# A decoder trunk on one core: the recurrence's decay computed from a tanh, and the order of the work around it

## What is computed

```
h = x * (1 + scale) + shift
proj = h @ w_in[l]                       # a_b a_c a_x a_g | q k v b_g | c_x c_g | d_u d_g
y_a = a_b * causal_dwconv(a_c * a_x) * silu(a_g)
y_b = dilated_attention(q, k, v, rel_bias) * silu(b_g)
y_c = rglru_branch(c_x, ...) * silu(c_g)
y_d = s5_branch(d_u, ...) * silu(d_g)
y = concat(y_a, y_b, y_c, y_d) @ w_out[l]
x = layer_norm(ALPHA * x + (1 + gate) * y)
```

```
r  = sigmoid(xh @ wa + ba);  ig = sigmoid(xh @ wx + bx)
log_a = -8 * r * softplus(-lam)
a = exp(log_a);  mult = sqrt(-expm1(2 * log_a))
h_t = a_t * h_(t-1) + mult_t * ig_t * xc_t
```

## Time and profile before

| | |
|---|---|
| Time, median of 3 runs | 1796.57 us (1792.95 to 1797.87) |
| The profiled execution | 1796.57 us, span 1794.8 us |
| Busy share of the span | TensorE 93%, its weight loads 72%, VectorE 68%, ScalarE 43%, POOL 13% |
| Mean granted clock of TensorE | 0.962 of full |
| First step of the loop of layer 0 and of layer 1: VectorE's start | 144.25 and 978.42 us |
| VectorE's start of the later steps, layer 0 | 299.37, 451.88, 605.27 us |
| VectorE's start of the later steps, layer 1 | 1135.47, 1286.36, 1437.29 us |

### The profile page before, as it was taken

The page is one execution under the profiler, slowest core; times in us unless marked ns, Lnnn a source line. Parts: engine busy times, 40 slices in busy tenths (PEclk is TensorE's granted clock), DMA queues, the critical chain, the costliest instruction groups (busy, mean ns, idle before and its releaser), DMA issues.

```text
span 1794.8 us, 23025 instructions
## 1 busy us (share of the span) xinstructions
PE 1666.7 (93%) x7527; PEld 1294.2 (72%) x7527; DVE 1219.8 (68%) x2338; ACT 774.2 (43%) x1022; POOL 233.3 (13%) x281
## 2 busy tenths in 40 slices
PE   2339999999999999999998999999999999999995
PEld 1327778777777777768886777877877777776884
DVE  5884894796688479657862576488468558743758
ACT  2125554653544555421127554554555464532120
POOL 2132111111111111000005111111111111100000
PEclk9559999999999999999997999999999999999998
DMA  7999889989988988858736788978988888855322
GB/s 255 369 349 254 212 208 241 231 222 229 222 223 209 237 227 213 237 166 292 224 121 178 178 187 205 221 185 188 218 198 195 198 203 193 186 166 206 134 95 104
DMA packets 322942, 376.05 MB, mean 210 GB/s; under 512 B 27064, under 2 KB 224032, under 8 KB 319784
## 3 DMA queue, kind: packets, MB, share of 16 engines
q1 hardware_dynamic: 294632, 272.36, 47.2%
q0 software_dynamic: 28224, 102.77, 31.9%
HBM read 261.81 MB, written 10.51 MB: 152 GB/s over the span
## 4 chain that ended last, share of the span: by engine, by line
PE 84%; DVE 8%; DMA 4%; ACT 2%; SPq 1%; issue 1%; POOL 0%; DVEq 0%; ACTq 0%; POOLq 0%
PE bank L970 19%; PE bank L977 19%; PE bank L971 18%; PE bank L1014 18%; DMA w_lo<-raw 3%; DVE work L1337 3%; DVE ada_acc L1337 2%; PE bank L860 2%; PE bank L994 2%; PE bank L890 1%; DVE y_t L1337 1%; PE bank L916 1%; PE bank L904 1%; PE bank L868 1%; PE bank L878 1%
## 5 line engine op out<-in xcount | busy, mean ns | idle before, releaser
L970 PE MATMUL bank<-op_hi,w_hi 128*128 128x512 f32 x1536 | 617.6, 402 | 0.0
L971 PE MATMUL bank<-op_lo,w_hi 128*128 128x512 f32 x1536 | 602.4, 392 | 0.0
L977 PE MATMUL bank<-op_hi,w_lo 128*128 128x512 f32 x1536 | 382.7, 391 | 7.4 <-DMA w_lo<-raw 7.4
L604 ACT ACTIVATE w_hi<-raw 128x1024 fp32r<-128x1024 f32 x196 | 207.8, 1060 | 399.1 <-PE bank L971 248.5
L970 PEld LDWEIGHTS bank<-op_hi,w_hi 128*128 128x128 f32 x1536 | 290.3, 189 | 94.2 <-issue 34.3
L977 PEld LDWEIGHTS bank<-op_hi,w_lo 128*128 128x128 f32 x1536 | 288.1, 188 | 71.6 <-DMA w_lo<-raw 12.2
L971 PEld LDWEIGHTS bank<-op_lo,w_hi 128*128 128x128 f32 x1536 | 290.4, 189 | 59.9 <-issue 1.9
L556 POOL DMA_DIRECT2D w_lo<-raw x196 | 170.9, 872 | 1056.2 <-ACT w_lo L607 1037.1
L607 ACT ACTIVATE w_lo<-raw 128x1024 fp32r<-128x1024 f32 x196 | 206.9, 1055 | 92.8 <-PE bank L977 92.7
L1337 DVE SCALAR_TENSOR_TENSOR ada_acc<-ada_in,cond,ada_acc 128x512 f32<-128x512 f32 (+1 forms) x234 | 181.5, 776 | 66.8 <-DMA ada_in<-in_w_ada 46.9
L744 ACT ACTIVATE w_hi<-raw 128x1024 fp32r<-128x1024 f32 x56 | 59.5, 1062 | 233.2 <-PE bank L1014 215.6
(11 more groups left out here) (226 smaller groups left out, 1568.5 us busy)
## 6 DMA issues: line engine op xcount, KB each, us to landing
w_lo<-raw POOLq DMA_DIRECT2D x196, 512.0 KB, 5.1
raw<-in_w_in SPq DMA_DIRECT2D x192, 512.0 KB, 4.4
ada_in<-in_w_ada SPq DMA_DIRECT2D x256, 256.0 KB, 4.4
raw<-in_w_out SPq DMA_DIRECT2D x64, 512.0 KB, 4.1
raw<-in_w_ada SPq DMA_DIRECT2D x27, 512.0 KB, 7.2
ada_in<-in_w_ada SPq DMA_DIRECT2D x18, 512.0 KB, 7.6
rot<-in_w_ada SPq DMA_DIRECT2D x10, 512.0 KB, 7.1
bias_t<-in_w_ada SPq DMA_DIRECT2D x9, 512.0 KB, 7.5
```

The costliest lines, as they stand in the source:

```text
L604: act.activation(w_hi[:, n % NHL, :], raw[:, n % NRAW, :], ACT.Copy).then_inc(s.hi_done.sem, 1)
L970: pe.matmul(o, w_hi[:, n % NHL, w], op_hi[:, k, :], start=k == 0, stop=False)
L971: mm = pe.matmul(o, w_hi[:, n % NHL, w], op_lo[:, k, :], start=False, stop=False)
L977: mm = pe.matmul(o, w_lo[:, n % NHL, w], op_hi[:, k, :], start=False, stop=k == KT - 1)
```

## The change

- ScalarE no longer computes the exponential. The square root of T goes to `lru_s[2]`, T itself stays in `lru_s[0]`.
- VectorE computes from T, with an addition, a reciprocal over 128x512, a product and one more `ts`: 1 / (1 + T), sqrt(T) / (1 + T) and a = 2 / (1 + T) - 1. The factor of `y_out(2)` goes from 0.25 to 0.5. The four columns of constants for the exponential go.
- TensorE: `s5_drive(3)` follows half-unit 13 instead of 14. It was put in the list ahead of the scores, so it runs before `scores(3)` there.
- VectorE's order: `s5_out(2)` comes before both `normalise`, an `ada` call between them, one more after `s5_scan(3)`; two calls near the end of the step go.
- SP: the S5 parameters of the next step are loaded behind everything of half 23 instead of at 22, and of the places for the conditioning's pieces one moves from 22 to 20 (the formula gives the same numbers for all others).

```diff
-ADA_AT = (1, 2, 4, 5, 7, 8, 10, 11, 13, 14, 16, 17, 19, 22, 22, 23)
-OWN_STEPS = (167, 166)
+ADA_PLACES = 16
+OWN_STEPS = (170, 169)
...
-                            if n == 22:
-                                s5_loads(step + 1)
-                        for place, at_half in enumerate(ADA_AT):
-                            if max(at_half, 2 - step) == n:
+                        for place in range(ADA_PLACES):
+                            if max(3 * place // 2 + 1, 1 + place, 2 - step) == n:
...
+                    if step < CT - 1:
+                        s5_loads(step + 1)
...
-                        act.activation(lru_s[2], lru_s[0], ACT.Exp, scale=lru_c[:, l, bass.ds(ct + 12, 1)],
-                                       bias=lru_c[:, l, bass.ds(ct + 12, 1)])
...
-                        act.activation(lru_s[0], lru_s[0], ACT.Sqrt).then_inc(s.from_act.sem, 1)
+                        act.activation(lru_s[2], lru_s[0], ACT.Sqrt).then_inc(s.from_act.sem, 1)
...
-                    for q, at in enumerate((5, 7, 10, 14)):
+                    for q, at in enumerate((5, 7, 10, 13)):
                         put(at, s5_drive, q)
...
                 dve.wait_ge(s.from_act.sem, s.from_act.at(2, ct))
-                own(stt(lru_s[0], lru_s[2], 1.0, lru_s[0], ADD, MUL), s.own)
+                own(ts(lru_s[0], lru_s[0], 1.0, ADD), s.own)
+                own(dve.reciprocal(lru_s[0], lru_s[0]), s.own)
+                own(tt(lru_s[2], lru_s[2], lru_s[0], MUL), s.own)
+                own(ts(lru_s[0], lru_s[0], 2.0, MUL, -1.0, ADD), s.own)
                 own(stt(lru_s[1], lru_s[1], 1.0, xc, ADD, MUL), s.own)
-                own(tt(lru_s[1], lru_s[1], lru_s[0], MUL), s.own)
-                own(dve.tensor_tensor_scan(xc, lru_s[2], lru_s[1], 0.0, MUL, ADD), s.own)
+                own(tt(lru_s[1], lru_s[1], lru_s[2], MUL), s.own)
+                own(dve.tensor_tensor_scan(xc, lru_s[0], lru_s[1], 0.0, MUL, ADD), s.own)
...
                 s5_scan(2)
                 ada(2, 1)
+                s5_out(2)
                 normalise(0)
+                ada(2, 1)
                 normalise(1)
-                s5_out(2)
                 own(silu2(0, "c_g", gx[:, 0, :]), s.own)
-                own(stt(y_out(2), xc, 0.25, gx[:, 0, :], MUL, MUL), s.gate_used[0])
+                own(stt(y_out(2), xc, 0.5, gx[:, 0, :], MUL, MUL), s.gate_used[0])
                 s5_in(3)
                 s5_scan(3)
+                ada(2, 1)
                 s5_out(3)
...
+
                 ada(2, 1)
-
                 own(silu2(0, "b_g", gx[:, 0, :]), s.own)
-                ada(2, 1)
-                ada(2, 1)
                 dve.wait_ge(s.pv_done.sem, s.pv_done.at(2 * ST, ct))
```

More of the change, by code:

```diff
@@ L172, in trunk @@
         s5c = sb("s5c", [P, DEPTH, 4, 16])
-        lru_c = sb("lru_c", [P, DEPTH, 16])
+        lru_c = sb("lru_c", [P, DEPTH, 12])
         glu_hb = sb("glu_hb", [P, DEPTH, 4])
@@ L1424, in preparation @@
                 own(ts(lru_c[:, :, 0:4], tmp[:, 3, :, 0:4], LRU_C / 4, MUL), sched)
-                own(ts(lru_c[:, :, 12:16], tmp[:, 3, :, 0:4], -LRU_C / 2, MUL), sched)
                 r = ROWS["lru_ba"][0]
```

## The result

The changed kernel takes 1821.8 us in the median of four runs (1820.3 to 1823.0) where the kernel before takes 1794.8 (1790.8 to 1797.9; the three runs of the table above and a fourth): a ratio of 1.0152, with a 95% interval of 1.0132 to 1.0172. It is 27 us slower. The forecast was 36.5 us slower (1833, range 1816 to 1848), so the measured time lies inside the range, in its lower part.

The account below looks back on a forecast made before the run. TensorE was taken as nearly always busy, with VectorE a hidden, almost level second bound in layer 0. Layer 0 23.8, layer 1 5.4, restarts 2.2 and clock 5.1 make 36.5 us on 1796.6: 1833, range 1816 to 1848.

Parts of the forecast that it names:

- The mechanism: In both layer loops, VectorE's later work makes TensorE wait where it needs VectorE's results: 1825 to 1841, chance 0.73.
- The wide reciprocal: VectorE's reciprocal over 512 columns, extrapolated from narrow rows: 3.35 us; net 4.3 us more on VectorE in each step.
- Layer 0: TensorE waits 1.7 after half 10, 1.25 after half 13, 3.0 after half 16: 5.95 us a step, 23.8 for four.
- Layer 1: TensorE waits 1.35 us a step before the second head's transposes after half 16: 5.4 us for four steps.
- The restart: Weights are not loaded ahead over a wait of TensorE: 16 waits x 0.14 = 2.2 us.
- The clock: Three of four waits of 3.0 us after half 16 are followed by a short fall to 1.2 GHz: 5.1 us.
- SP's queue: S5 loads behind the last half's loads, one ada place from half 22 to 20; TensorE doesn't wait there: 0.
- The cheap reciprocal: Rival: the wide reciprocal takes 0.43 us; layer 0 waits 13.4 us in all, layer 1 5.4: 1822, chance 0.08.
- That the clock falls at every wait: Rival: TensorE's clock falls at every wait, longer after the long ones, 20.4 us instead of 5.1: 1848, chance 0.12.
- The rival of a faster kernel: Rival: shifted loads relieve the start of a step, where w_lo came late, giving back 6.7 us: 1790, chance 0.03.

Follow-up runs that it names:

- the cheap reciprocal: The changed kernel with the reciprocal replaced by a multiplication with 0.5 over the same 128x512, which changes the recurrence's values: 1814.8 us, 1.0104 to the kernel before.
- the try: The kernel before with the S5 loads behind half 23 and the third and fourth ada places at halves 5 and 6 instead of 4 and 5: 1787.6 us, 0.9958.

## Why the forecast came out as it did

**The mechanism held.** VectorE is an almost level second bound in layer 0; TensorE waits for it at fixed meeting points. The new waits stand where they were forecast and nowhere else: after halves 10, 13 and 16 in layer 0, after half 16 in layer 1, none before the S5 outputs. The arithmetic alone, the order alone, and the changed kernel with the exponential back each show their own part of these waits.

**Term by term.**
- *The wide reciprocal:* 3.35 us from three narrow rows; measured 3.353. The slope of the rows held over 480 more columns. The Trainium skill ("VectorE: DVE Perf Modes", the walkthrough, fixed hardware budget) gives a repeat count of 8; taken as 8 cycles a column, that was an estimate of 4.3 us. The trace disagrees with that reading of it. (By the forecast's own steps it would have raised the sum by 0.9 us a step in layer 0, so by some 4 us and not by 6.)
- *Layer 0, forecast 5.95 us a step (1.7, 1.25, 3.0).* Measured 1.46, 0.83 and 2.77, so 5.06 where all three stand, 18.6 over four steps against 23.8. At the first bank release VectorE is 2.36 us late (365.45 against 355.55, with TensorE 7.54 later in the two traces), not 2.6, so the first wait is 0.2 shorter. Before the second, the kernel before had a pause of 0.48 us in VectorE's step, ahead of the first piece of the second ada chunk (371.90), and the changed kernel has none there. I had carried it over. In the first and the fourth step the second wait is missing: the clock had fallen behind the first, and the slower TensorE took it up.
- *Layer 1, forecast 1.35 us a step.* Measured 1.82, 7.3 us in all. With the exponential back it is 1.37. With the cheap reciprocal it is 1.82 still, so it is not VectorE's lateness. The difference is a pause of 0.48 us ahead of the ada piece between the normalises (1252.87 above), which is missing with the exponential back.
- *The restart, forecast 2.2 us:* at most a part of it is there. From the first S5 outputs to the second, layer 0 takes 157.96 us against 153.10. That is 4.86 more, with 5.06 of new waits and 0.46 less for w_lo, so 0.26 us are left for three waits where 0.42 were forecast. In layer 1 the second step grew by 1.68 us with a wait of 1.82, so nothing is left. Behind its wait the first transpose takes 0.33 us where it took 0.27 before (409.87 above, 397.08 in the earlier trace rows); the next half-unit's first matmul takes 0.48 us in both kernels.
- *The clock, forecast 5.1 us:* behind the long waits it lost 3.4 + 1.7 = 5.1. That the number fits is luck: not three short falls but a short and a long one, and behind the same four waits the order alone lost 8.5 and the exponential back 6.7. Behind the waits after half 10 it fell twice more, 3.4 us lost; the second wait that is missing in these two steps made up for half of that.
- *SP's queue, taken as 0:* right for the two together. But that was luck too, for a reason that I hadn't named. The place at half 20 is harmless only because VectorE takes a pair between the normalises; alone it costs 20 us. My argument (asked for well ahead, TensorE doesn't wait there) looked at the S5 loads and not at the ring.

The sum of the measured is smaller than its parts. The waits are 25.9 us, the falls behind them lost 5.1 + 3.4 = 8.5, and the waits for w_lo got shorter by 1.1 over the span: 33.3 against the 27.6 of the span. What is missing is in the clock elsewhere. Added up over the whole span in stretches of 10 us, the low clock loses 69.1 us before and 71.9 in the changed kernel, so only 2.8 more. The fall of the earlier trace rows at 748 (1.7 us) has no counterpart in the changed kernel, and around the turn from layer 0 to layer 1 (first line before, second line changed) it loses 8.4 us instead of 13.8:

```profile
940.00:1000.00 60.00, 51.22 (x219) 40.78 (x218) 14.95 (x37) 37.99 (x51) 24.69 (x21) 0.77 0.67 174
```
```profile
965.00:1025.00 60.00, 50.38 (x234) 40.03 (x234) 17.02 (x39) 42.84 (x56) 25.70 (x22) 0.86 0.74 183
```

With 2.8 for the clock the sum is 25.9 + 2.8 - 1.1 = 27.6. From the last S5 outputs of layer 0 to the first of layer 1 the kernel before takes 378.6 us and the changed one 375.0, in spite of a new wait of 1.8. The kernels of the experiments take 372 to 380 there, those without any new wait on the way among them. So this part looks like spread between executions and not like something that the change did; no run separates it.

**The rivals.** The cheap reciprocal was forecast at 1822 and measured, as its own kernel, at 1815: there was no wait after half 13 where I had 0.4 us a step (1.6 in all) and next to nothing for restarts (1.7), but 7.3 us of waits in layer 1 where I had 5.4; the waits for w_lo were 2.4 us shorter over the span. The rest of the 7 us is open. That the clock falls at every wait didn't happen: it fell behind none of the waits of 1.4 to 1.8 us in layer 1, and behind 13 of 16 of 2.8 us in layer 0 over four kernels (the changed one, the order alone, the cheap reciprocal, the exponential back). The rival of a faster kernel was no answer to this change, but its place was real: the waits for w_lo at the start of layer 0's steps are those that the try took away.

## What to carry to other kernels

List the points at which the bounding engine takes something from another, and write the slack at each: what is added ahead of a point costs in full less the slack there, as the waits of these runs show, and nothing as long as it stays under the slack. Waits at two points of one chain replace each other, so price the parts together: here 8 (the arithmetic), 19 (VectorE's order), 0 (the drive) and 20 us (SP's queue) alone are 27 in one kernel. A load placed in an in-order queue carries the wait for its slot to everything behind it, so a place must be moved with the consumer that frees the slot.

## What the hardware showed that I had not expected

- VectorE pauses for about half a microsecond at one or two places of a step without any releaser that explains it (0.48 us at 371.90 before, 0.53 at 1234.43 before, 0.48 at 1252.87 after). The place moves when instructions are added or taken ahead of it. It moved the waits of this case by 0.4 to 0.5 us a step, both ways. The wait of 0.3 us after half 13 goes with it too: the drive alone has the pause (371.68) and the wait, the cheap reciprocal has neither. What the pause is was not tested.
- The same wait isn't always followed by a fall of TensorE's clock. Behind waits of 2.8 us it fell to 1.2 GHz in 13 of 16 cases, mostly for 3.4 us; behind waits of 3.3 to 3.4 before the S5 outputs (the ada calls, with and without the new queue) in only 4 of 8; behind waits of 1.46 us after half 10 in 6 of 12; behind 1.24 us (s5_out(2) alone) and 1.4 to 1.8 us (layer 1) in none of 16. The cause of the difference was not found. It may also make part of the spread of a few us between runs of one kernel; that is a guess.
